# Projection stage of a decoder step on one core: x also taken in turned from memory, and the sample's rows multiplied with high and low parts side by side

## What is computed

```
def rms_norm(x, g, eps=NORM_EPS):
    xf = x.astype(jnp.float32)
    y = xf * lax.rsqrt(jnp.mean(xf * xf, axis=-1, keepdims=True) + eps)
    return (y * g.astype(jnp.float32)).astype(x.dtype)

def project(h, w_in):
    p = h @ w_in          # 1024 -> 3072: q, k, v of group A, then of group B
    ...
```

## Time and profile before

| | |
|---|---|
| median of 3 runs | 1261.97 us (1261.82 to 1265.04) |
| the profiled execution, its own time | 1260.89 us |
| its span in the trace | 1259.1 us |
| TensorE busy | 1142.3 us (91%) |
| VectorE, ScalarE, GpSimd busy | 699.0, 597.0, 141.0 us |
| mean granted clock of TensorE | 0.967 |
| projection stage | 0 to about 331 us |

### The profile page before, as it was taken

How to read it: one execution, slowest core, us unless ns; L and a number is a source line. 1 busy time by engine, 2 the same in 40 slices (tenths; PEclk the granted TensorE clock), 3 DMA queues, 4 the chain that set the end, 5 groups by cost and what they waited for, 6 DMA issues and landing times. The chain is left out here.

```text
span 1259.1 us, 23319 instructions
## 1 busy us (share of the span) xinstructions
PE 1142.3 (91%) x7695; PEld 821.1 (65%) x7695; DVE 699.0 (56%) x1048; ACT 597.0 (47%) x1030; POOL 141.0 (11%) x172
## 2 busy tenths in 40 slices
PE   7999999999789889959889999998499999999992
PEld 6877888888445556635555667876367666667771
DVE  4322112220167767658798996543566766666664
ACT  5530122201176767637466664222165655556654
POOL 1100000000011111100000000000123222333311
PEclk9999999999899999979999999999599999999997
DMA  6642243317599999999999955433679999875476
GB/s 209 217 133 77 83 146 126 100 42 250 197 366 381 381 365 332 380 369 381 382 376 383 318 210 174 161 125 117 265 276 363 377 378 292 235 173 115 100 217 193
DMA packets 155392, 307.43 MB, mean 244 GB/s; under 512 B 22311, under 2 KB 49354, under 8 KB 151178
## 3 DMA queue, kind: packets, MB, share of 16 engines
q1 hardware_dynamic: 145018, 272.38, 60.1%
q0 software_dynamic: 9216, 33.56, 11.3%
q10 hardware_dynamic: 1040, 0.00, 0.0%
HBM read 308.31 MB, written 54.72 MB: 288 GB/s over the span
## 5 line engine op out<-in xcount | busy, mean ns | idle before, releaser
L327 PE MATMUL proj_ps<-w_in_split,x_T_hi 128*128 128x512 f32 x608 | 194.5, 395 | 2.7 <-DVE w_in_split L369 2.7
L2516 DVE TENSOR_TENSOR w_gate_up_split<-w_gate_up,w_gate_up_split 128x2048 fp32r<-128x2048 f32 x62 | 139.3, 2288 | 84.5 <-ACT w_gate_up_split L2574 84.5
L2467 PE MATMUL gate_up_ps<-w_gate_up_split,slot_rows_T 128*128 128x512 f32 x744 | 177.7, 394 | 3.3 <-DVE slot_rows_T L2524 3.3
L2467 PEld LDWEIGHTS gate_up_ps<-w_gate_up_split,slot_rows_T 128*128 128x128 f32 x744 | 137.4, 188 | 32.2 <-DVE slot_rows_T L2524 4.5
L327 PEld LDWEIGHTS proj_ps<-w_in_split,x_T_hi 128*128 128x128 f32 x608 | 115.0, 189 | 27.7 <-DVE x_T_lo L364 2.5
L455 ACT ACTIVATE proj_rows<-proj_ps,sum_squares 128x512 f32<-128x512 f32 x38 | 26.2, 689 | 211.5 <-PE proj_ps L327 199.7
L327 PE MATMUL proj_ps<-w_in_split,x_T_lo 128*128 128x512 f32 x304 | 119.1, 392 | 0.0
L2574 ACT ACTIVATE w_gate_up_split<-w_gate_up 128x2048 fp32r x62 | 115.3, 1913 | 4.7 <-DMA w_gate_up<-in_w_up 3.1
L2489 PE MATMUL expert_out_ps<-w_down,expert_act_T 128*128 x256 | 115.3, 593 | 0.2 <-issue 0.2
L1736 PE MATMUL mix_out_ps<-w_out_split,oT_split 128*128 128x512 f32 x420 | 101.2, 396 | 0.3 <-DVE w_out_split L1875 0.3
L1142 PE MATMUL turns_and_scores_ps<-head_kT,head_qT 64*128 64x512 f32 (+3 forms) x384 | 81.8, 537 | 15.7 <-issue 10.7
(11 more groups left out here) (255 smaller groups left out, 1733.1 us busy)
## 6 DMA issues: line engine op xcount, KB each, us to landing
w_gate_up<-in_w_gate SPq DMA_DIRECT2D x34, 1024.0 KB, 8.4
w_gate_up<-in_w_up SPq DMA_DIRECT2D x34, 1024.0 KB, 10.2
w_down<-in_w_down SPq DMA_DIRECT2D x34, 1024.0 KB, 12.2
pages<-in_cache_v_d SPq DMA_DIRECT2D x128, 256.0 KB, 5.8
pages<-in_cache_kT_s SPq DMA_DIRECT2D x128, 256.0 KB, 5.2
pages<-in_cache_v_s SPq DMA_DIRECT2D x128, 256.0 KB, 5.1
pages<-in_cache_kT_d SPq DMA_DIRECT2D x100, 256.0 KB, 5.9
w_in_now<-in_w_in SPq DMA_DIRECT2D x48, 256.0 KB, 3.1
```

The costliest lines, as they stand in the source:

```text
L327: last = pe.matmul(pj_ps[:, n % PJ_BANKS, :], h[:, k, at], w[g % 2][:, k, :], start=(k == 0 and m == 0), stop=(k == KC - 1 and m == 2))
L2467: last = pe.matmul(gu_ps[:, u, :], xT[:, u, a, k, :], gu_split[:, u, b, k, :], start=(k == 0 and m == 0), stop=(k == KC - 1 and m == 2))
L2516: dve.tensor_tensor(gu_split[:, u, 1, at, :].rearrange("p k (c n) -> p k c n", c=2), raw[:, at, :, :], gu_split[:, u, 0, at, :].bitcast(F3 ...
```

## The change

- **x turned, from memory.** A second input `xT` holds each tile of x already turned. `load_xT(n)` loads it (512 KB) into one of `XT_PLACES` = 2 places; `high_x` and `low_x` read it from there. `turn_x` and its 72 transposes are gone.
- **x in rows, one place.** x in rows is still loaded, for `square` alone, now into a single place (`x_tile`, before 3 places): `load_x(n)` waits until `square(n-1)` is done. In step n of group 0 SP now issues `load_xT(n+2)` and `load_x(n+2)`, where before it issued `load_x(n+3)`.
- **The sample's tile.** Rows 64 to 127 of tile 8 no longer hold zeros: of `x_T_hi` columns 0 to 63 of the tile are the high parts, columns 64 to 127 the low parts of the same 64 rows. One matmul with the weights' high part gives high*high in rows 0 to 63 and low*high in rows 64 to 127; with the weights' low part the second product. So the six steps of the sample's tile have 16 matmuls each, before 24. `fold_rows` on VectorE scales both halves of the result and adds them (two instructions of 64x512), where ScalarE's `keep_rows` did it with one. The sample's stores and transposes have 64 rows or columns, before 128.

The diff, cut to its core:

```
-        x = sb("x_tiles", [P, X_PLACES, D_MODEL])
+        x_T = sb("x_T_tiles", [P, XT_PLACES, KC, P])
+        x = sb("x_tile", [P, D_MODEL])
...
+        def row_free(engine, r):
+            if r >= 3:
+                engine.wait_ge(rows_stored[r % 3], 16 * len([s for s in row_stores[r % 3] if in_rows[s] < r]))
+                if by_row[r - 3] in turned:
+                    engine.wait_ge(tr_done, turned[by_row[r - 3]] + 1)
...
+                def load_xT(n):
+                    if n >= TILES:
+                        return
+                    if n >= XT_PLACES:
+                        sp.wait_ge(lo_done, 2 * (n - XT_PLACES) + 2)
+                    sp.dma_start(x_T[:, n % XT_PLACES, :, :], t.xT[n].rearrange("p (k c) -> p k c", c=P))\
+                      .then_inc(xT_loaded[n % XT_PLACES], 16)
+
                 def load_x(n):
-                    if n >= X_PLACES:
-                        sp.wait_ge(xT_done, 2 * (n - X_PLACES) + 2)
-                        sp.wait_ge(squares, n - X_PLACES + 1)
-                    sp.dma_start(x[:, n % X_PLACES, :], t.x[n * P:(n + 1) * P, :]).then_inc(x_loaded[n % X_PLACES], 16)
+                    if n >= TILES:
+                        return
+                    if n:
+                        sp.wait_ge(squares, n)
+                    sp.dma_start(x[:, :], t.x[n * P:(n + 1) * P, :]).then_inc(x_loaded, 16)
...
-                load_x(0)
+                load_xT(0)
                 for k in range(KC):
                     load_w(0, k)
-                    if k in (2, 5):
-                        load_x(k // 2)
+                    if k == 2:
+                        load_xT(1)
+                    if k == 5:
+                        load_x(0)
+                load_x(1)
                 tables.loads(sp)
...
-                        if g == 0 and n + X_PLACES < TILES:
-                            load_x(n + X_PLACES)
+                        if g == 0:
+                            load_xT(n + XT_PLACES)
+                            load_x(n + 2)
...
-                        if n == 0 and k == 3:
-                            turn_x(1)
...
-                            for m, (h, w) in enumerate(((hT_hi, w_hi), (hT_lo, w_hi), (hT_hi, w_lo))):
+                            pairs = ((hT_hi, w_hi), (hT_lo, w_hi), (hT_hi, w_lo)) if a < PT else ((hT_hi, w_hi), (hT_hi, w_lo))
+                            for m, (h, w) in enumerate(pairs):
...
-                    if g == 0 and n + 2 < TILES:
-                        turn_x(n + 2)
...
+                    low = hT_lo[:, at, cols] if n < PT else hT_hi[:, at, PT * P + N_SAMPLE:PT * P + 2 * N_SAMPLE]
+                    dve.tensor_tensor(low, x_T[:, n % XT_PLACES, at, 0:live(n)], hT_hi[:, at, cols].bitcast(F32),
+                                      ALU.subtract).then_inc(lo_done, 1)
...
+                def fold_rows(step):
+
+
+                    n, r = number[step], in_rows[step]
+                    high, low = slice(0, N_SAMPLE), slice(N_SAMPLE, 2 * N_SAMPLE)
+                    dve.wait_ge(pj_done, n + 1)
+                    if step[0] == 0:
+                        dve.wait_ge(rstd, PT + 1)
+                    dve.tensor_scalar_mul(low_rows[step[0] > 0], pj_ps[low, n % PJ_BANKS, :], ss[low, 2, PT:PT + 1]).then_inc(low_taken, 1)
+                    row_free(dve, r)
+                    dve.wait_ge(rows_kept, r)
+                    dve.wait_ge(low_taken, folded.index(step) + 1)
+                    dve.scalar_tensor_tensor(proj[high, r % 3, :], pj_ps[high, n % PJ_BANKS, :], ss[high, 2, PT:PT + 1], low_rows[step[0] > 0],
+                                             ALU.mult, ALU.add).then_inc(rows_kept, 1)
...
-                    act.wait_ge(xT_done, m + 1)
+                    act.wait_ge(xT_loaded[n % XT_PLACES], 16 * (n // XT_PLACES + 1))
...
-                    act.wait_ge(x_loaded[n % X_PLACES], 16 * (n // X_PLACES + 1))
+                    act.wait_ge(x_loaded, 16 * (n + 1))
...
+                    if r and by_row[r - 1] in folded:
+                        act.wait_ge(rows_kept, r)
```

More of the change, by code:

```diff
@@ L106 @@
 BY_ROWS = len(CHUNKS)
-X_PLACES = 3
+XT_PLACES = 2
 PJ_BANKS = 3
@@ L184, in project, with live @@
         tables = Tables(nc, ctx, sems, t, [xT_ps[:, n, :] for n in range(2)], by_distance)
+        by_row = list(in_rows)
+        def live(n):
+            return P if n < PT else N_SAMPLE
+        def row_free(engine, r):
[3 more added lines that the diff above has]
+                    engine.wait_ge(tr_done, turned[by_row[r - 3]] + 1)
         def last_of(g):
@@ L213, in store_rows @@
                     dst, at = (t.new_kvd, t.new_kvs)[kind], (ROLE_COLS[role] - 1) * HALF_W
-                    sp.dma_start(dst[tile * P:(tile + 1) * P, at:at + HALF_W], proj[:, r % 3, :])\
+                    rows = P if tile < PT else N_SAMPLE
+                    sp.dma_start(dst[tile * P:tile * P + rows, at:at + HALF_W], proj[0:rows, r % 3, :])\
                       .then_inc(rows_stored[r % 3], 16)
@@ L296, in turn_k @@
                         pe.wait_ge(tr_kept, n - 2)
+                    rows = P if step[1] < PT else N_SAMPLE
                     for b in range(4):
-                        last = pe.transpose(tr_ps[:, n % 3, b * P:(b + 1) * P], proj[:, r % 3, b * P:(b + 1) * P],
-                                            t.ident[:, :])
+                        last = pe.transpose(tr_ps[:, n % 3, b * rows:(b + 1) * rows], proj[0:rows, r % 3, b * P:(b + 1) * P],
+                                            t.ident[0:rows, 0:rows])
                     last.then_inc(tr_done, 1)
@@ L408, in _ @@
                         keep_columns(step)
+                    if step in folded:
+                        fold_rows(step)
                     if at < KC and g + 1 < len(GROUPS):
@@ L449, in keep_rows @@
                         act.wait_ge(rstd, tile + 1)
[L450 to L454, removed]
+                    row_free(act, r)
+                    if r and by_row[r - 1] in folded:
+                        act.wait_ge(rows_kept, r)
                     act.activation(proj[:, r % 3, :], pj_ps[:, n % PJ_BANKS, :], ACT.Copy, scale=ss[:, 2, tile:tile + 1])\
@@ L487, in _ @@
                         keep_across(at)
-                    if step in in_rows:
+                    if step in in_rows and step not in folded:
                         keep_rows(step)
                     if g == 0:
+                        if n == PT:
+                            act.wait_ge(rstd, PT + 1)
                         diagonal(n)
```

51 lines of the change are left out of this document (21 added, 30 removed).

## The result

The change makes the kernel slower: 1279.69 us (median of 4 runs, 1276.67 to 1284.87) against 1262.73 us (median of 4, 1261.82 to 1265.04) on the same chip, a ratio of 1.0134 with the interval 1.0113 to 1.0155, so 17 us or 1.3%, well clear of none. Forecast were 1269.1 us, 8.2 more than before, and a range of 1260 to 1278: the sign and the mechanism are right, the size is 9 us too small, and the median lies outside the range. The profiled execution took 1277.76 us, its span is 1276.0; it is 16.9 us longer than the span of before.

A forecast was written before the change was run, and what follows sets the result against it. TensorE bounds the projection stage; in group 0 a 9.0 us load loop would take over. Group 0 +16.6, later groups -9.2, fold +0.8 make +8.2 on 1260.9: 1269.1 us, range 1265 to 1276, 8 in 10 1260 to 1278.

The forecast's parts named there:

- The closed ring: Group 0: SP's issue of turned x, landing, ScalarE, VectorE, back to SP; 9.0 us a step, against 6.81 before.
- S + 5.0: Group 0: x in rows lands 5.0 us after S, SP's issue of the turned x; bounds 3.7 and 7.4.
- The first step: Group 0: from SP's issue of turned x in step 0 at 21.1 us to that in step 1 at 30.1.
- S(0): Start of group 0: SP issues step 0's turned x at 21.1 us, behind ten small loads taking 4.2 us.
- one slow landing: Group 0: one landing 2.4 us later than the median, raising the group's lengthening from 14.2 to 16.6 us.
- The later groups: Groups 1 to 5: each sample step loses 8 matmuls, 1.84 us, giving 9.2 us in all.
- The end of the stage: End of group 5: the fold's two VectorE instructions replace ScalarE's one, adding 0.8 us; 0 to 1.5 possible.
- The weights of group 1: Start of group 1: part 7 ready at 88.8 us, wanted by TensorE at 91.1, so nothing added.
- Rival 1: Group 0: both loads land side by side, loop 7.7 us; 1257.6 us, or about 1263 with half; chance 0.15.
- rival 2: Group 0 stays bound by TensorE, the loop falling below 5.94 us; 1244.6 us; chance 0.07.
- Rival 3: Group 0: TensorE's clock at half through whole products, 1283 us, chance 0.08; if partly, under 2 us, called likelier.
- all landings at 6.1: Group 0: every landing at 6.1 us would add 14 us, 1283 in total; left out of the range.

The follow-up runs named there:

- e4: Changed kernel, group 0: keep_rows, diagonal and weights ahead of x's parts and square on ScalarE and VectorE, SP's weights load ahead of x's loads; 1255.2 us.
- e8: Changed kernel without the load of x in rows, squares summed over the turned tile instead, so other numbers result; 1265.9 us.
- e10: Changed kernel with SP's weights load, before right behind the two x loads, issued only after the store of rows; 1304.3 us.
- e6: Changed kernel with SP's stores of rows and turned keys in group 0 issued a step late, behind the loads of x and weights; 1282.7 us.
- e7: Changed kernel with the ten small table loads ahead of the load of x's tile 1 at the start; 1274.9 us.
- e1: Kernel before with only the sample's half: 16 matmuls a sample step and fold_rows, x loaded and turned as before; 1252.0 us.
- e5: Changed kernel with both loads of x issued from ScalarE's queue, not SP's, x in rows behind the square, turned x behind the diagonal; 1256.1 us.
- e9: Changed kernel with rows first on ScalarE and VectorE, weights ahead of x on SP, and table loads ahead of x's tile 1; 1253.9 us.
- e3: Changed kernel with only ScalarE's and VectorE's order altered in group 0: keep_rows, diagonal and weights ahead of x's parts and square; 1278.6 us.

## Why the forecast was right in kind and too small

- **What bounds the kernel, and what becomes the bound.** This was right. The closed ring of SP, landing, ScalarE, VectorE and SP is there as forecast, in the order forecast, and TensorE idles in it. e4 shows it by taking the ring apart with all bytes kept, e8 by taking the bytes away with the ring kept. The links behind the landing were 4.0 us forecast and 3.8 measured.
- **The step that failed is one term of the sum, the landing: "so it lands at S + 5.0".** It was S + 6.2 in the mean. The steps from S(1) to S(6) took 50.5 us (31.93 to 82.46), for 45. I had priced two loads in a row with the median landing of one load and the transfer rate of the busiest microsecond. Both parts were too small: the turned x itself landed 4.6 us after S in the mean of six steps (3.75 to 5.31), for 3.7, and x in rows 1.7 us behind it, for 1.3. In e8, without the second load, the turned x took 4.1. Why two loads in this surrounding take 6.2 us stays open (e10 and e6 above).
- **The first step, 11.7 us and not 9.0.** S(0) = 21.1 was near (20.25), but S(1) came at 31.93: the turned x, issued right behind the ten small loads, took 6.5 us to land, and x in rows 7.5. Those loads were counted as time of SP's queue only, and not as work for the transfers behind them. That they are the cause is likely and not isolated: from 20 to 23 us the queues moved 25 GB/s, and in e7, where the small loads stand elsewhere, the turned x issued at 16.44 landed in 4.4 us and x in rows issued at 20.78 in 3.4; but e7 also pulls these two loads apart.
- **The sum.** Start -0.9, first step +2.7, five steps +5.5, last part +0.9 make 8.2, and group 1 begins at 94.55 for 86.3. Of that the forecast had provided 2.4 as one slow landing. The later groups give back 22.4 - 13.95 = 8.5 us (344.07 against 330.12), forecast 9.2; e1 shows the same gain alone. The end of the stage costs 1.2 more for 0.8. Behind the stage the attention and the rest are 1.7 us longer, which I did not look into, since the medians move by that much.
- **The weights of group 1** did not add, as forecast: part 7 was ready at 97.8, inside the first product.
- **Rival 1** (loads side by side) and **rival 2** (TensorE stays the bound) are out: the loads came slower than reckoned, not faster. Rival 2's time is what e4, e5 and e9 approach once the ring is broken, but 9 to 12 us above it.
- **Rival 3, TensorE's clock.** The part that I called likelier came: the clock fell to 0.80 to 0.83 in group 0 (windows above), where each step has a gap of 1.9 to 3.0 us. The first matmuls of a step run at half clock (0.43 us from one start to the next, later 0.23) and are hidden: TensorE still waits in every step, and the last product, the only one that nothing covers, ran at full clock and took 3.7 us. The Trainium skill, "TensorE: Matmul & The Clock Gate", HAM oscillation, is borne out in that the clock falls in such a rhythm; in the changed kernel it cost nothing, because TensorE was not what the steps waited for. In e4 it cost 2.8 us.
- **The range** was too narrow above. The bounds of the landing itself held but for the first step: S + 6.2 lies between S + 3.7 and S + 7.4. But the range did not carry them through. It allowed for one to three slow landings, and in the trace all seven came later than 5.0, the first 7.9 us after S and the others 5.8 to 6.9; and it left out the case of "all landings at 6.1", whose 1283 us lie nearer to the result than the forecast.

## What to carry to other kernels

Before a load is moved into the step that uses it, follow the ring: what does the issue wait for in its queue, who waits for the landing, and does that lead back to the same queue? Every link of such a ring costs its full time in every step, here the landing most of all with 6.2 of 10 us, and removing one link can leave another ring of nearly the same length (e3). Keep loads a step ahead, put what closes a short ring ahead of what is only bulk (e4), or issue the loads from a queue in which they do not wait behind stores (e5). And where two loads are added next to each other and no row shows such a pair, take the bound of the landing through every step into the range.

If one wants the gain, the sample's half alone (e1, 0.9938) or the whole with the three orders changed (e9, 0.9925) both beat the kernel before; these two cannot be told apart by their intervals. So x turned from memory, even in the best of these orders, shows no gain over leaving x as it was.

## What the runs showed of the hardware that I had not expected

- Landings of back-to-back loads could not be added up from one load and a rate: one load of 512 KB took 3.7 us at the median, and the second of two, issued 0.5 us behind the first, was used 5.7 us after the first one's issue in e10 and 6.2 us after it in the changed kernel, for 5.0 by such a sum.
- A load of 512 KB issued right behind ten small loads (51 KB and less each) took 6.5 us, and the queues moved 25 GB/s from 20 to 23 us, before it got going. In e7, without the small loads right ahead, it took 4.4 us.
- A copy of 512 KB between two places of the main memory, issued behind the loads, did not stretch them (6.1 us for 6.2 in the changed kernel).
